# Attention on one Trainium2 core: value matmuls of two heads alternated on column halves, 64-row score products on row halves

## The reference

```python
# first block, twice: 8 heads, query and key of 64 + 32 columns, 512 keys, no mask, value of 64
s = jnp.einsum('bqhd,bkhd->bhqk', qb, k); p = softmax(s); o = jnp.einsum('bhqk,bkhd->bqhd', p, v)
# second block, cross attention: 4 heads of 64 over 256 memory tokens
# second block, 16 heads of 64 in 4 groups, a sum of three gated branches
#   o_c over 31 compressed keys; o_s over selected blocks; o_w over a window
return g_b[..., 0:1] * o_c + g_b[..., 1:2] * o_s + g_b[..., 2:3] * o_w
```

## Time and profile before

| | |
|---|---|
| median of three runs | 3654.3 us |
| profiled execution: span | 3654.2 us, within 0.1 us of that median |
| TensorE busy | 3361.3 us (92%) |
| VectorE busy | 1827.6 us (50%) |
| mean granted TensorE clock | 0.948 |
| first attention, two times | 668 to 753 us, 1822 to 1907 us |
| cross attention | 2622 to 2666 us |
| compressed attention | 2947 to 2987 us |
| two-branch attention | 2988 to 3229 us |

### The profile page before, as it was taken

The page is one execution under the profiler, slowest core; times in us unless marked ns, Lnnn a source line. Parts: engine busy times, 40 slices in busy tenths (PEclk is TensorE's granted clock), DMA queues, the critical chain, the costliest instruction groups (busy, mean ns, idle before and its releaser), DMA issues.

```text
span 3654.2 us, 38427 instructions
## 1 busy us (share of the span) xinstructions
PE 3361.3 (92%) x14296; PEld 2546.8 (70%) x14296; DVE 1827.6 (50%) x2505; ACT 698.3 (19%) x1441; POOL 1609.6 (44%) x834
## 2 busy tenths in 40 slices
PE   6999889989999999988999999878799889989998
PEld 5888655568887888764467888556567756668886
DVE  4323694644235323388554313477435167756435
ACT  2001211431001100111151101233311125531101
POOL 4666520036666666641005666444335400036665
PEclk9999989999999999988999999888799959999999
DMA  3323320012223232321002323221112300013222
GB/s 115 112 84 103 109 72 6 1 47 92 98 92 98 86 104 92 98 97 55 6 1 75 109 87 100 79 66 56 63 59 81 107 24 1 1 47 104 90 89 75
DMA packets 65485, 263.13 MB, mean 72 GB/s; under 512 B 7390, under 2 KB 8606, under 8 KB 63808
## 3 DMA queue, kind: packets, MB, share of 16 engines
q1 hardware_dynamic: 61344, 238.86, 20.3%
q10 hardware_dynamic: 4000, 22.37, 1.7%
HBM read 259.10 MB, written 2.10 MB: 71 GB/s over the span
## 4 chain that ended last, share of the span: by engine, by line
PE 75%; DVE 19%; ACT 2%; issue 2%; DMA 1%; ACTq 0%; POOL 0%; DVEq 0%; SPq 0%; POOLq 0%
PE psum L490 18%; PE psum L492 18%; PE psum L491 18%; PE psum L569 4%; PE psum L601 3%; DVE y_conv L1721 2%; DVE full L1551 2%; PE psum L586 2%; PE psum L709 2%; PE psum L724 2%; PE psum L667 2%; PE psum L508 1%; DVE xc L1949 1%; DVE htmp L1554 1%; PE psum L806 1%
## 5 line engine op out<-in xcount | busy, mean ns | idle before, releaser
L458 POOL TENSOR_SCALAR w_hi<-w_raw 128x1024 fp32r<-128x1024 f32 (+2 forms) x415 | 478.9, 1154 | 1987.3 <-PE psum L492 1971.2
L460 POOL TENSOR_TENSOR w_lo<-w_raw,w_hi 128x1024 fp32r<-128x1024 f32 (+2 forms) x415 | 1130.5, 2724 | 34.6
L490 PE MATMUL psum<-u_hi,w_hi 128*128 128x512 f32 x2584 | 1039.4, 402 | 37.7 <-DVE u_lo L1436 31.3
L491 PE MATMUL psum<-u_lo,w_hi 128*128 128x512 f32 x2584 | 1017.9, 394 | 0.0
L492 PE MATMUL psum<-u_hi,w_lo 128*128 128x512 f32 x2584 | 1016.8, 393 | 0.0
L490 PEld LDWEIGHTS psum<-u_hi,w_hi 128*128 128x128 f32 x2584 | 493.3, 191 | 175.3 <-issue 48.3
L491 PEld LDWEIGHTS psum<-u_lo,w_hi 128*128 128x128 f32 x2584 | 493.8, 191 | 109.0 <-issue 9.4
L492 PEld LDWEIGHTS psum<-u_hi,w_lo 128*128 128x128 f32 x2584 | 492.4, 191 | 105.1
L490 PE MATMUL psum<-h_hi,w_hi 128*128 128x512 f32 x960 | 374.4, 390 | 5.7 <-DVE h_lo L1561 5.2
L492 PE MATMUL psum<-h_hi,w_lo 128*128 128x512 f32 x960 | 373.5, 389 | 0.0
L491 PE MATMUL psum<-h_lo,w_hi 128*128 128x512 f32 x960 | 373.5, 389 | 0.0
(11 more groups left out here) (273 smaller groups left out, 3522.2 us busy)
## 6 DMA issues: line engine op xcount, KB each, us to landing
w_raw<-in_w SPq DMA_DIRECT2D x335, 512.0 KB, 3.5
w_raw<-in_w SPq DMA_DIRECT2D x48, 768.0 KB, 4.2
w_raw<-in_w SPq DMA_DIRECT2D x32, 640.0 KB, 3.9
dft<-in_dft ACTq DMA_DIRECT2D x2, 2048.0 KB, 12.8
idft<-in_idft ACTq DMA_DIRECT2D x2, 2048.0 KB, 7.9
w_c<-in_w_c ACTq DMA_DIRECT2D x2, 2048.0 KB
x<-in_xt SPq DMA_DIRECT2D x1, 2048.0 KB, 8.5
decay<-in_decay ACTq DMA_DIRECT2D x2, 1024.0 KB, 6.9
```

The source lines that it names most:

```text
L458: pool.tensor_scalar(hi, raw, 1.0, 1.0, ALU.mult, ALU.mult).then_inc(w_hi_ready, 1)
L460: pool.tensor_tensor(lo, raw, hi.bitcast(F32), ALU.subtract).then_inc(w_split, 1)
L490: pe.matmul(out, hi[:, c, :], rhs_hi(c), start=(s == 0), stop=False)
L491: pe.matmul(out, hi[:, c, :], rhs_lo(c), start=False, stop=False)
```

## The change

The unit lists are reordered: for each block of queries the even and the odd head of a pair of heads follow each other. V is now done for two units together, in the odd steps: for each branch and each block of keys one product of the even head, then one of the odd head, so that successive products write different column halves. Where query and key have 64 rows (cross and two-branch attention, not the first attention with 96), S is done for two units together in the even steps, after that step's transposes, branch by branch and head by head, so that successive products read different row halves; both wait until the exponentials of all earlier units are done. There are four buffers of transposed probabilities in place of two, and ScalarE waits for V of the unit four before. The compressed attention keeps its order. VectorE's program is unchanged.

```diff
-        pt = [mid(f"pt{i}", [P, 1, TB, P], U_AT + 2 * i * K1) for i in range(2)]
+        pt = [mid(f"pt{i}", [P, 1, TB, P], U_AT + 2 * i * K1) for i in range(4)]
...
-        ptx = [mid(f"ptx{i}", [P, 1, TB, P], R_AT + (16 + 2 * i) * K1) for i in range(2)]
+        ptx = [mid(f"ptx{i}", [P, 1, TB, P], R_AT + (16 + 2 * i) * K1) for i in range(4)]
...
-        pt2 = [mid(f"pt2{i}", [P, 2, TB, P], H_AT + (40 + 4 * i) * K1) for i in range(2)]
+        pt2 = [mid(f"pt2{i}", [P, 2, TB, P], (H_AT + 40 * K1, U_AT + 16 * K1)[i // 2] + 4 * (i % 2) * K1)
+               for i in range(4)]
...
+            kw["alone"] = kw["kind"] == "cmp"
+            kw["halves"] = kw["kind"] != "cmp" and kw["qk"][0][1].shape[0] == HD
...
-                    for h in range(HEADS) for i in ORDER]
+                    for hp in range(0, HEADS, 2) for i in ORDER for h in (hp, hp + 1)]
...
-                    for h in range(XHEADS) for i in ORDER]
+                    for hp in range(0, XHEADS, 2) for i in ORDER for h in (hp, hp + 1)]
...
                 for i in ORDER:
                     n = P * (i + 1)
+                    for h in (hp, hp + 1):
...
                 for s in range(len(units) + VALUES):
-                    if s < len(units):
+                    halves = s < len(units) and units[s]["halves"]
+                    if s < len(units) and not halves:
                         u = units[s]
...
+                    if halves and s % 2 == 0:
+
+                        if s >= 2:
+                            pe.wait_ge(exp_done, p0 + parts_of(units, s))
+                        for b in range(len(units[s]["qk"])):
+                            for e in range(2):
+                                u = units[s + e]
+                                _, q, key = u["qk"][b]
+                                mm = pe.matmul(score[e][:, b, 0:u["n"]], q, key, start=True, stop=True,
+                                               skip_group_check=True)
+                                if b == len(u["qk"]) - 1:
+                                    mm.then_inc(s_full, 1)
+                    if s >= VALUES and units[s - VALUES]["alone"]:
                         u, k = units[s - VALUES], u0 + s - VALUES
...
+                    elif s >= VALUES and (s - VALUES) % 2 == 1:
+
+                        both = [(units[s - VALUES - 1 + e], u0 + s - VALUES - 1 + e) for e in range(2)]
+                        pe.wait_ge(t_taken, p0 + parts_of(units, s - VALUES + 1))
+                        if both[0][0]["opens"] and w.item >= 2:
+                            pe.wait_ge(o_taken, w.item - 1)
+                        nb_, nc_ = len(both[0][0]["v"]), len(both[0][0]["v"][0])
+                        for b in range(nb_):
+                            for c in range(nc_):
+                                last = b == nb_ - 1 and c == nc_ - 1
+                                for u, k in both:
+                                    mm = pe.matmul(product[w.item % 2][u["rows"], P * u["i"]:P * u["i"] + P],
+                                                   u["v"][b][c], u["pt"][k % 4][:, b, c, :],
+                                                   start=(b == 0 and c == 0), stop=last, skip_group_check=True)
+                                    if last:
+                                        mm.then_inc(pv_done, 1)
...
-                        if k >= 2:
-
-                            act.wait_ge(pv_done, k - 1)
+                        if k >= 4:
+
+                            act.wait_ge(pv_done, k - 3)
```

More of the change, by code:

```diff
@@ L369, in cross_units @@
                          v=[[vx[:, j, HD * h:HD * h + HD] for j in range(MEM // P)]])
-                    for h in range(XHEADS) for i in ORDER]
+                    for hp in range(0, XHEADS, 2) for i in ORDER for h in (hp, hp + 1)]
         def nsa_units(compressed):
             out = []
[L375 to L378, removed]
+            for hp in range(0, HEADS2, 2):
+                g = hp // (HEADS2 // GROUPS)
                 if compressed:
[L380 to L386, removed]
+                    out.append(unit(head=hp, i=None, kind="cmp", scale=HD ** -0.5, n=None, keep=prob2, pt=pt2,
+                                    qk=[(i, q2[:, hp // 2, P * i:P * i + P],
+                                         k_cmp[:, g, :, :].rearrange("p e n -> p (e n)")) for i in range(TB)],
+                                    v=[v_cmp[:, g, :, :].rearrange("p e c -> p (e c)")],
+                                    gate=gates[:, :, 3 * hp:3 * hp + 6]
+                                    .rearrange("p t (e k) -> p t e k", k=3)[:, :, :, 0]))
                     continue
@@ L389, in nsa_units @@
                     n = P * (i + 1)
[L390 to L394, removed]
+                    for h in (hp, hp + 1):
+                        r = slice(HD * (h % 2), HD * (h % 2) + HD)
+                        q = q2[r, h // 2, P * i:P * i + P]
+                        out.append(unit(head=h, i=i, kind="pair", scale=HD ** -0.5, n=n, keep=prob2, pt=pt2,
+                                        qk=[(b, q, k2[r, b, g, 0:n]) for b in range(2)],
+                                        v=[[v2[:, b, j, g // 2, HD * (g % 2):HD * (g % 2) + HD]
+                                            for j in range(i + 1)] for b in range(2)],
+                                        gate=gates[:, i, 3 * h + 1:3 * h + 3]))
             return out
@@ L587, in attention @@
                             mm.then_inc(t_full, 1)
-                    if s >= VALUES:
+                    if halves and s % 2 == 0:
[9 more added lines that the diff above has]
+                                    mm.then_inc(s_full, 1)
@@ L589, in attention @@
+                    if s >= VALUES and units[s - VALUES]["alone"]:
                         u, k = units[s - VALUES], u0 + s - VALUES
-                        buf = u["pt"][k % 2]
                         out = product[w.item % 2][u["rows"], :]
                         pe.wait_ge(t_taken, p0 + parts_of(units, s - VALUES + 1))
-                        if u["opens"] and w.item >= 2:
+                        if w.item >= 2:
                             pe.wait_ge(o_taken, w.item - 1)
[L595 to L604, removed]
@@ L605, in attention @@
-                        mm.then_inc(pv_done, 1)
-                        if u["closes"]:
+                        pe.matmul(out, u["v"][0], u["pt"][k % 4][0:2 * CPAD, 0, :, :].rearrange("p c q -> p (c q)"),
+                                  start=True, stop=True, skip_group_check=True).then_inc(pv_done, 1)
+                        w.item += 1
+                    elif s >= VALUES and (s - VALUES) % 2 == 1:
[13 more added lines that the diff above has]
+                                        mm.then_inc(pv_done, 1)
+                        if both[1][0]["closes"]:
@@ L1072, in attention @@
                             nch, rows = len(u["chunks"]), u["chunks"][0][1]
-                            act.activation(u["pt"][k % 2][0:rows, b, 0:nch, :],
+                            act.activation(u["pt"][k % 4][0:rows, b, 0:nch, :],
                                            turned[(p + b) % 2][0:rows, 0:P * nch]
```

## The result

The changed kernel takes 3715.5 us (median of four runs, 3713.6 to 3716.8) against 3653.6 for the kernel before, timed beside it: a ratio of 1.0168, 95% interval 1.0156 to 1.018. The forecast was 3715. The profiled execution has a span of 3714.5 us.

The account below looks back on a forecast made before the run. TensorE was taken to bound the first and cross attention, a ring of waits through three engines the two-branch attention. The sum was 3654 - 17 - 8 + 89 = 3718 us, stated as 3715, range 3655 to 3785.

Parts of the forecast that it names:

- the likeliest case: Whole kernel: overlap happens and the two-branch clock falls and rises; 3676 to 3760 us, chance 0.45.
- first attention, both layers: First attention: overlapped value matmuls shorten two units from 5.02 to 4.48 us, 32 times, -17 us.
- cross attention: Cross attention at the low clock: two units take 4.61 us against 5.62, 8 times, -8 us.
- two-branch attention: Two-branch attention: two heads take 39.6 us against 28.44, +89 us.
- pairs a = 1 to 4, high to low clock: Two-branch attention: time per pair of units with a blocks of keys, summing to 34.35 us at 2.4 GHz, 44.9 at 1.2.
- Overlap in the halves: Matmuls in different array halves run side by side; n dependent matmuls take n/2 + 1 passes of 0.11 us at high clock.
- The joint wait: Two-branch attention: paired scores lose double buffering; the ring of successive steps through three engines takes 34.35 us per two heads, +47.
- The clock: Two-branch attention: TensorE waits of 2.4 to 3.3 us lower its clock; middle of 34.35 and 44.9 us taken, +89.
- no overlap: Rival: matmuls in different halves do not overlap; +7, -3 and +87 us give 3745 at 2.4 GHz, chance 0.18.
- clock holds: Rival: overlap, with the two-branch attention staying at 2.4 GHz; -17 - 8 + 47 = +22, 3676 us, chance 0.20.
- faster: Rival: two-branch ring cheaper, down to VectorE's own work, 23.4 us per two heads; 3589 us, decided below 31.6, chance 0.11.
- nothing: Rival: two-branch period near 31.6 us per two heads, so the gains cancel; 3654 us, chance 0.06.

Follow-up runs that it names:

- experiment 1: Changed kernel with two-branch scores issued one unit per step again, each waiting only for the exponentials of the unit two before: 3651.7 us.
- the filler: Changed kernel plus six products whose result is never used behind each pair of scores in the two-branch attention: 3692.0 us.
- experiment 8: Changed kernel plus six 128-column products without use behind each pair of two-branch scores, where TensorE waits: 3692.0 us.
- experiment 12: Kernel with only the two-branch order of heads changed (3661 us), plus four useless products behind scores with four blocks of keys: 3648.6 us.
- old two-branch attention: Changed kernel with two-branch attention put back: head after head, scores and values one unit per step, four buffers staying: 3626.3 us.
- late values: Changed kernel with two-branch attention put back as before, and values of two units one step later in first and cross attention: 3603.2 us.

## Why the prediction was right

The time, the sign and the likeliest case (the clock goes up and down) came out. By its own steps:

| step | forecast | measured |
|---|---|---|
| first attention, both layers | -17 | -20.6 |
| its period for two units | 4.48 | 4.42 |
| cross attention | -8 | -7.1 |
| its period for two units | 4.61 | 4.46 |
| two-branch attention | +89 | +88.0 |
| its period for two heads | 39.6 | 40.7 (38.1 once in six) |
| pairs a = 1 to 4, high to low clock | 7.0 to 10.4, 7.55 to 10.8, 9.85 to 11.4, 10.0 to 12.3 | 8.96, 8.62, 10.53, 12.62 |

**Overlap in the halves** was right, whole, for rows and columns. It takes n/2 passes and not the n/2 + 1 that I counted: the 16 loads pass in the time of eight, so the two matmuls of a product are no obstacle. That one pass, 0.11 us at the high and 0.21 us at the low clock, is as much as the periods of the first (0.06) and the cross attention (0.15) came out shorter, or more.

**The rule of the Trainium skill** (TensorE: Matmul & The Clock Gate, The mechanism), that a weight load overlaps matmuls in flight only in another group of rows, doesn't hold here: between column halves, which share all rows, 16 loads pass in 0.85 us beside 16 matmuls. The same section also names a background weight buffer as a way for a load to be pulled ahead; whether that is what happens here no run shows. The same section's rule that tiles overlap agrees with the trace.

**The joint wait** was right as the largest cost: +64 us by experiment 1. The sum of its ring, 34.35 us per two heads at the high clock, was never seen by itself, since no run with that wait held the clock. What there is goes its way: 40.7 us at a clock of 0.71, 38.1 at 0.78, and with the filler 36.0 at 0.91. Three of the four pairs in the trace lie between my numbers for the two clocks, that of a = 4 a little above (12.62 against 12.3). Behind S of the pairs a = 1 to 4 TensorE waits 2.69, 3.27, 3.44 and 4.02 us for its transposes, where I had 2.4 to 3.3, and between S of a = 3 and S of a = 4 it waits another 2.04 us, which I didn't have.

**The clock** was right in kind, shown by experiments 8 and 12. Its 42 us were only the middle of two bounds; the 23 us of the filler are a lower bound. That the time lay near the middle I couldn't know: that the forecast of +89 met +88.0 so closely is luck.

**What the prediction didn't have** is a cost of the order of the heads. It took the order as free ("a is one less, 4 before 1" was all that it did in the ring) and gave the whole +47 us to the wait, and the clock's loss with it. The runs divide the 89 us otherwise: from the old two-branch attention (3626) the order adds 35, values in halves take off 10 (3652), the joint wait adds 64 (3715.5). So the stage was sized right as a whole (the ring's sum was made for the new order and the new wait together), but what I wrote of its cause put another edit's cost on the wait. The order's own cost at a full clock is small (at most 1.2 us per two heads, experiment 12). What I missed is that the clock already falls by the order alone, to 0.82, where the waits for the transposes are only 1.0 to 1.7 us. The three steps add up in this sequence of edits; since each has a part of the clock in it, another sequence could divide them otherwise.

The rival "no overlap" falls by the 16 loads in 0.85 us, "clock holds" by the window's 0.70, "faster" and "nothing" by the 40.7 us, which lie above the deciding 31.6.

## What to carry to other kernels

Halves of the array do double the pace of small matmuls, but only where TensorE is what the stage waits for: the change gained 28 us in two stages that had it busy throughout, and lost 89 us in one that ran on a ring through three engines (values in halves alone took 10 us off there). There, pairing two units so that their matmuls can overlap took the double buffering away and was dearer than all the overlap gave. Before a loop is reordered for overlap, add up the ring with the new waits, and ask what the longer idle time does to TensorE's clock; and put the paired work where its operands have long been ready (late values: another 23 us).

## What the runs showed of the hardware

- Products of one half that follow four matmuls of the other start beside them without being alternated in the program (eight score matmuls in 1.14 us in either order), while of eight and eight about four overlap (1.58 us for 16, against 1.09 alternated).
- Useless matmuls made a program faster: 384 of them in the idle places of one stage took 23 us off and raised the granted clock from 0.70 to 0.85.
- The same instructions and waits in another order of units cost 35 us of 3626, with TensorE busy for 249 us in place of 217. Most of it is the granted clock: two heads take 34.2 us at 0.80, and 29.6 us at 1.00 even with useless matmuls added.
